# Forgetting attention in an encoder block: two heads at a time on the two halves of the TensorE array

## What is computed

```
scale = q.shape[-1] ** -0.5
cum = jnp.cumsum(log_f, axis=-1)
for blk in range(s // Q_BLOCK):            # Q_BLOCK = 128, s = 512
    lo = blk * Q_BLOCK
    hi = lo + Q_BLOCK
    logits = (einsum("bhtd,bhsd->bhts", q[:, :, lo:hi], k[:, :, :hi]) * scale
              + (cum[:, :, lo:hi, None] - cum[:, :, None, :hi]))
    mask = (lo + arange(Q_BLOCK))[:, None] >= arange(hi)[None, :]
    p = softmax(where(mask, logits, -inf), axis=-1)
    outs.append(einsum("bhts,bhsd->bhtd", p, v[:, :, :hi]))
```

## Time and profile before

| | us |
|---|---|
| median of three runs | 819.95 |
| profiled execution, span from first to last instruction | 818.3 |
| TensorE busy | 805.7 (98%) |
| VectorE busy | 371.3 (45%) |
| ScalarE busy | 255.4 (31%) |
| attention stage, from the first L1319 to the last gate piece | 95.1 |

### The profile page before, as it was taken

The page is one execution under the profiler, slowest core; times in us unless marked ns, Lnnn a source line. Parts: engine busy times, 40 slices in busy tenths (PEclk is TensorE's granted clock), DMA queues, the critical chain, the costliest instruction groups (busy, mean ns, idle before and its releaser), DMA issues.

```text
span 818.3 us, 9506 instructions
## 1 busy us (share of the span) xinstructions
PE 805.7 (98%) x3851; PEld 652.7 (80%) x3851; DVE 371.3 (45%) x573; ACT 255.4 (31%) x421; POOL 24.0 (3%) x43
## 2 busy tenths in 40 slices
PE   6999999999999999999999999999999999999996
PEld 6988887888665578888888988888888888888885
DVE  4688334357654443424435534434443443323224
ACT  6444211343433323323324333322333223213211
POOL 4000000012000000000000000000000000000001
PEclk9999999999999999999999999999999999999999
DMA  8434342311010103533331333322233332331402
GB/s 225 126 99 145 103 129 77 103 52 31 22 52 1 52 1 103 206 103 103 103 103 52 92 115 103 103 89 80 90 102 103 104 103 83 123 103 52 155 0 103
DMA packets 61915, 75.63 MB, mean 92 GB/s; under 512 B 3680, under 2 KB 49840, under 8 KB 61872
## 3 DMA queue, kind: packets, MB, share of 16 engines
q1 hardware_dynamic: 61872, 75.02, 28.9%
HBM read 72.92 MB, written 2.10 MB: 92 GB/s over the span
## 4 chain that ended last, share of the span: by engine, by line
PE 94%; DMA 2%; DVE 1%; issue 1%; ACT 1%; SPq 0%; POOL 0%; POOLq 0%; ACTq 0%; DVEq 0%
PE bank L1136 27%; PE bank L1138 27%; PE bank L1137 27%; PE bank L1319 3%; PE bank L1339 3%; PE bank L1260 2%; DMA x_nat<-in_x 1%; PE bank L1327 1%; PE bank L1299 1%; DMA stage<-in_w_in 1%; PE bank L1286 1%; DVE work L783 0%; DVE w_lo L722 0%; PE bank L1279 0%; PE bank L1148 0%
## 5 line engine op out<-in xcount | busy, mean ns | idle before, releaser
L1136 PE MATMUL bank<-hT_hi,w_hi 128*128 128x512 f32 (+1 forms) x680 | 261.6, 385 | 2.7 <-DVE hT_lo L706 2.5
L1138 PE MATMUL bank<-hT_hi,w_lo 128*128 128x512 f32 (+1 forms) x680 | 257.1, 378 | 0.0
L1137 PE MATMUL bank<-hT_lo,w_hi 128*128 128x512 f32 (+1 forms) x680 | 257.0, 378 | 0.0
L722 DVE TENSOR_TENSOR w_lo<-stage,w_hi 128x1024 fp32r<-128x1024 f32 x125 | 152.4, 1224 | 223.0 <-ACT w_hi L464 214.3
L464 ACT ACTIVATE w_hi<-stage 128x1024 fp32r<-128x1024 f32 x127 | 133.3, 1052 | 132.8 <-PE bank L1138 125.5
L1136 PEld LDWEIGHTS bank<-hT_hi,w_hi 128*128 128x128 f32 x680 | 128.9, 190 | 26.1 <-POOL w_lo L407 2.8
L1138 PEld LDWEIGHTS bank<-hT_hi,w_lo 128*128 128x128 f32 x680 | 128.7, 189 | 23.7
L1137 PEld LDWEIGHTS bank<-hT_lo,w_hi 128*128 128x128 f32 x680 | 128.8, 189 | 21.6
L1136 PE MATMUL bank<-w_hi,aT_hi 128*128 128x512 f32 x176 | 68.5, 389 | 0.0
L1137 PE MATMUL bank<-w_lo,aT_hi 128*128 128x512 f32 x176 | 68.5, 389 | 0.0
L1138 PE MATMUL bank<-w_hi,aT_lo 128*128 128x512 f32 x176 | 68.5, 389 | 0.0
(11 more groups left out here) (169 smaller groups left out, 821.3 us busy)
## 6 DMA issues: line engine op xcount, KB each, us to landing
stage<-in_w_in SPq DMA_DIRECT2D x21, 1024.0 KB, 5.2
stage<-in_w_gate SPq DMA_DIRECT2D x11, 1024.0 KB, 5.3
stage<-in_w_up SPq DMA_DIRECT2D x11, 1024.0 KB, 5.3
stage<-in_w_down SPq DMA_DIRECT2D x22, 512.0 KB, 4.4
stage<-in_w_out SPq DMA_DIRECT2D x4, 1024.0 KB, 5.0
x_nat<-in_x SPq DMA_DIRECT2D x4, 512.0 KB, 5.4
stage<-in_w_br_mlstm SPq DMA_DIRECT2D x4, 512.0 KB, 3.5
stage<-in_w_br_fox SPq DMA_DIRECT2D x4, 512.0 KB, 4.6
```

Source lines behind the costliest of these rows:

```text
L722: dve.tensor_tensor(ring(w_lo, g), staged(g), ring(w_hi, g).bitcast(F32), ALU.subtract).then_inc(lo_split, 1)
L1136: pe.matmul(o, a_hi, b_hi, start=first, stop=False)
L1137: pe.matmul(o, a_hi, b_lo, start=False, stop=False)
L1138: return pe.matmul(o, a_lo, b_hi, start=False, stop=last)
```

## The change

Units are replaced by 16 pairs v: the two heads of a head pair for one query block. `fox_pair(v)` goes through q = 0, 1, 2, 3, 3, 2, 1, 0 twice. For a pair TensorE issues both query-key products (head 0 on array rows 0 to 63, head 1 on rows 64 to 127, into two banks), both row products, and both masks; then, per key block, the value products of the two heads in turn. The row product now uses 64 array rows as well: `rows_both` is copied to partitions 64 and up (three VectorE copies, `rows_low_half`), and `pick` gets a second set of ones by two more `affine_select` on GpSimd (N_CONSTS 17 to 19). There are four `probs` tiles, four logit banks (4, 5, 6, 1), one result bank (0) for all head pairs, and the last head's transpose moves from bank 1 to bank 7. Each pair has two gate pieces from v = 2 on, so 28 of the 32 lie in the loop and 4 behind it; before it was 31 and 1.

```diff
-            def fox_logits(u):
-                hp, q, h2 = fox_unit(u)
...
-                bank, n = 4 + u % 3, (q + 1) * P
-                head = slice(h2 * DH_F, (h2 + 1) * DH_F)
-                take(bank, (fox_exp, u + 1))
-                pe.matmul(psum[bank][:, 0:n], q_f[head, hp, q * P:(q + 1) * P], k_f[head, hp, 0:n], start=True, stop=False)
-                spread_row(bank, H_M + 2 * hp + h2, q, False, True).then_inc(logits, 1)
+            def fox_logits(v):
+                hp, q = fox_pair(v)
+                if v == 0:
...
+                    pe.wait_ge(rows_low_half, 3)
...
+                for h2 in range(2):
+                    take(logit_bank(2 * v + h2), (fox_exp, 2 * v + h2 + 1))
+                for h2, head in enumerate(heads):
+                    pe.matmul(banks[h2][:, 0:n], q_f[head, hp, q * P:(q + 1) * P], k_f[head, hp, 0:n],
+                              start=True, stop=False)
+                for h2, head in enumerate(heads):
+                    lane = H_M + 2 * hp + h2
+                    pe.matmul(banks[h2][:, 0:n], pick[head, lane:lane + 1].to_broadcast([DH_F, P]), rows_both[head, cols],
+                              start=False, stop=False)
+                for h2 in range(2):
+                    pe.matmul(banks[h2][:, q * P:n], ident_b[:, :], mask_b[:, :], start=False,
+                              stop=True).then_inc(logits, 1)
...
+            def fox_values(v):
+                hp, q = fox_pair(v)
...
+                for h2 in range(2):
+                    pe.wait_ge(fox_PT[h2], v + 1)
+                if v % ROWS == 0:
+                    take(0, (yfT_lo_ready, hp + 1))
                 for j in range(q + 1):
-                    last = pe.matmul(psum[hp % 2][h2 * DH_F:(h2 + 1) * DH_F, q * P:(q + 1) * P],
-                                     v_f[:, j, c:c + DH_F], work[u % 2][:, j * P:(j + 1) * P],
-                                     start=(j == 0), stop=(j == q))
+                    for h2 in range(2):
+                        c = (2 * hp + h2) * DH_F
+                        last = pe.matmul(psum[0][h2 * DH_F:(h2 + 1) * DH_F, q * P:(q + 1) * P],
+                                         v_f[:, j, c:c + DH_F], work[h2][:, j * P:(j + 1) * P],
+                                         start=(j == 0), stop=(j == q))
                 last.then_inc(fox_pv, 1)
...
-            for u in range(2, 35):
...
+            for v in range(FOX_PAIRS):
+                fox_transpose(v)
+                if v + 2 < FOX_PAIRS:
+                    fox_logits(v + 2)
+                if v == 0:
+                    mlstm_transpose(3)
+                if v >= FILL_FROM:
+                    gate_piece(2 * (v - FILL_FROM))
+                fox_values(v)
+                if v >= FILL_FROM:
+                    gate_piece(2 * (v - FILL_FROM) + 1)
```

VectorE, at granule `G_MV + 2`, behind the three subtractions that finish `rows_both`:

```diff
+                    for n, (a, b) in enumerate(ROW_CHUNKS):
+                        dve.wait_ge(rows_lo_ready, n + 1)
+                        dve.tensor_copy(rows_both[HALF_ARRAY:HALF_ARRAY + LO + LANES, a * P:b * P],
+                                        rows_both[0:LO + LANES, a * P:b * P].bitcast(F32)).then_inc(rows_low_half, 1)
```

VectorE, the attention stage (ScalarE's loop goes by pairs in the same way, with `take_yfT_hi` and the gate's `tanh` at the head of an iteration):

```diff
+            fox_row_max(0)
+            head_mean_square(3)
+            fox_divide(0)
+            fox_row_max(1)
+            head_normalise(3)
+            take_ymT(2)
+            for v in range(FOX_PAIRS):
+                fox_take_even(v)
+                if v >= ROWS and v % ROWS == 0:
+                    take_yfT_lo(v // ROWS - 1)
+                if v + 1 < FOX_PAIRS:
+                    fox_divide(v + 1)
+                if v + 2 < FOX_PAIRS:
+                    fox_row_max(v + 2)
+                if v == 0:
+                    open_gate(3)
+                if v == 1:
+                    take_ymT(3)
+                if v in (2, 3):
+                    split_lo(G_BR + v)
+                if v in (6, 10):
+                    split_lo(G_BR + 4 + (v - 6) // 4)
```

More of the change, by code:

```diff
@@ L195, in block_kernel @@
         rows_both = at("rows_both", [P, 10 * P], F32R, R + 72 * K)
-        probs = [at(f"probs{i}", [P, SEQ], F32, R + 82 * K + 2 * K * i) for i in range(3)]
+        probs = [at(f"probs{i}", [P, SEQ], F32, R + 80 * K + 2 * K * i) for i in range(4)]
         mo_half_tanh = at("mo_half_tanh", [P, SEQ], F32, R + 70 * K)
@@ L399, in _ @@
                                      base=0, pattern=[[1, P]], channel_multiplier=-1))
+            for at_row in (HALF_ARRAY, HALF_ARRAY + LO):
+                const(pool.affine_select(out=pick[:, H_M:LANES], in_=pick[:, H_M:LANES].bitcast(F32),
+                                         compare_op=ALU.not_equal, fill=1.0, base=-at_row - H_M,
+                                         pattern=[[-1, H_F]], channel_multiplier=1))
+                pool.wait_ge(consts, steps[0])
             assert steps[0] == N_CONSTS
@@ L592, in _ @@
             act.wait_ge(decay_exp, 10 * H_M)
[L593 to L608, removed]
-                if n in (0, 1) and (u - FILL_FROM) % KD == 2:
-                    split_hi(G_BR + 4 + n)
-                if u in (6, 8):
-                    split_hi(G_BR + 2 + (u - 6) // 2)
-                if u >= 8 and u % 8 == 4:
-                    take_yfT_hi(u // 8 - 1)
+            fox_softmax(0)
+            fox_softmax(1)
+            mo_tanh_of(3)
+            take_ymT_hi(2)
+            act.wait_ge(y_m, H_M)
+            for v in range(FOX_PAIRS):
+                if v >= ROWS and v % ROWS == 0:
+                    take_yfT_hi(v // ROWS - 1)
+                if v > FILL_FROM and v % 4 == FILL_FROM:
+                    first_gate_tanh(v // 4 - 1)
+                fox_take_odd(v)
+                if v in (2, 3):
+                    split_hi(G_BR + v)
+                if v + 2 < FOX_PAIRS:
+                    fox_softmax(v + 2)
+                if v == 1:
+                    take_ymT_hi(3)
+                if v in (6, 10):
+                    split_hi(G_BR + 4 + (v - 6) // 4)
             take_yfT_hi(KB - 1)
@@ L987, in fox_take_even @@
+            def fox_take_even(v):
+                _, q = fox_pair(v)
                 n = (q + 1) * P
[L988 to L990 removed]
+                dve.wait_ge(fox_T, 2 * v + 1)
+                if v >= 1:
+                    dve.wait_ge(fox_pv, v)
                 dve.tensor_copy(work[0][:, 0:n], psum[2][:, 0:n]).then_inc(fox_PT[0], 1)
[L993 to L1006 removed]
+            fox_row_max(0)
@@ new lines, in fox_logits @@
+                n = (q + 1) * P
+                cols = slice(pair(q, 0) * P, pair(q, 0) * P + n)
+                banks = [psum[logit_bank(2 * v + h2)] for h2 in range(2)]
+                heads = [slice(h2 * DH_F, (h2 + 1) * DH_F) for h2 in range(2)]
+                for h2 in range(2):
[3 more added lines that the diff above has]
+                              start=True, stop=False)
@@ new lines, in fox_logits, with fox_transpose @@
+                for h2, head in enumerate(heads):
+                    lane = H_M + 2 * hp + h2
+                    pe.matmul(banks[h2][:, 0:n], pick[head, lane:lane + 1].to_broadcast([DH_F, P]), rows_both[head, cols],
+                              start=False, stop=False)
+                for h2 in range(2):
+                    pe.matmul(banks[h2][:, q * P:n], ident_b[:, :], mask_b[:, :], start=False,
+                              stop=True).then_inc(logits, 1)
+            def fox_transpose(v):
+                _, q = fox_pair(v)
+                for h2 in range(2):
+                    u = 2 * v + h2
+                    pe.wait_ge(fox_norm, 2 * u + 2)
+                    take(2 + h2, (fox_PT[h2], v + 1))
+                    for j in range(q + 1):
+                        last = pe.transpose(psum[2 + h2][:, j * P:(j + 1) * P], probs[u % 4][:, j * P:(j + 1) * P], ident[:, :])
+                    last.then_inc(fox_T, 1)
```

155 lines of the change are left out of this document (59 added, 96 removed).

## The result

| | before | after |
|---|---|---|
| median of runs, us | 819.87 (4 runs) | 797.97 (4 runs, 797.34 to 798.50) |
| ratio to before | | 0.9733, 95% interval 0.9722 to 0.9744 |
| profiled execution, span | 818.3 | 796.5 (run time 798.42) |
| attention stage | 95.1 | 73.5 |

The account below looks back on a forecast made before the run. The prediction took TensorE's own instruction list as the bound. Its terms, -5.9 - 3.6 - 2.3 - 6.9 + 2.5 + 0.5 = -15.7 us, brought the span from 818.3 to 802.6, forecast as 804 for a run, range 798 to 818.

Parts of the forecast that it names:

- What bounds the kernel: Whole kernel and attention stage: only TensorE's own list can give time; TensorE is busy for 805.7 of 818.3 us.
- Term 1: Attention units: array shape changes fall from 96 to 64 at 0.184 us each, saving 5.9; counted by fixed parts, 8.8.
- Term 2: Query-key products on two row halves: four slots become three, saving 4.3, less 0.7 for weight loads: net 3.6 us.
- Term 3: Row products: the first head's stands beside the second head's last query-key instruction, saving 2.3 of 4.6 us.
- Term 4: Value products in turn on two column halves: 4(q + 1) slots become 2(q + 1) + 1, saving 6.9 us.
- Term 5: Start of the attention stage: TensorE waits for bank 1 and VectorE's chain, costing 2.5 us (bounds 0 to 4).
- Item 6: Steady state of the pairs: VectorE's work is covered by TensorE's; only the gate tanh at v = 14 costs 0.5 us.
- Item 7: Three VectorE copies at 79 us and two more GpSimd constants: cost 0; without cover 1.6 and 0.6 us.
- The rival with two slots: Query-key and value products: the pair runs as one, two slots instead of three; 799 us, chance 0.04.
- The other side: Logits and values: every change of half costs like a change of shape; 837.5 us, 827 at half price; chance 0.12.

Follow-up runs that it names:

- e8: The kernel after, with the two row products of a pair on all 128 array rows instead of on halves; 800.34 us.
- e1: The kernel after, with a pair's value products issued head by head instead of in turn; 801.58 us.
- e3: The kernel after, with query-key and row products of both heads taken from array rows 0 to 63 (second head's logits wrong); 808.31 us.
- e2: The kernel after, with value products of both heads sent to the same 64 columns (attention result wrong); 805.60 us.
- e7: The kernel after, with value products issued in groups of two key blocks per head; 798.44 us.
- e5: The kernel after, with ScalarE's tanh of bank 3 ahead of pair 1's exponentials and pair 1's logits behind all four pieces of that block; 798.02 us.
- e9: e5's order, with VectorE's starting list changed (division before mean square, head 2's step behind the first copy) and the last head's transposes one pair later; 798.05 us.
- e10: e5's order with pair 0's division ahead of the mean square, gate pieces from pair 0 on, and the last two mLSTM heads' transposes moved off bank 7; 799.48 us.
- e12: e10 with VectorE's copy for the first values ahead of the last mLSTM head's normalise step, and ScalarE's gate tanh ahead of its result copy; 796.17 us.
- e11: The kernel after, unchanged, run again on the same chip as e10; 798.49 us.

## Why the prediction was right and wrong

- **What bounds the kernel**: right. Nearly all of the gain is TensorE's list in that stage.
- **Term 1, changes of shape** (-5.9): right in kind. By the rows after, a pair has 0.21 fixed in the logits, 0.15 in the values, and 0.09 to 0.11 at each of three borders to full-array work: about 0.65 where two units had 1.11, so -7.3 over 16 pairs. No run takes this part away alone; the stage without waits and half clock fell by 27.2, of which terms 2 to 4 as measured below are 19.5, which leaves 7.7. The term counted four changes at one price, and the return ahead of the bf16 mask is cheaper than ahead of the row product (0.21 against 0.31; e8).
- **Term 2, query-key products** (-3.6): the step that failed. "TensorE starts in order: A1, then A2 beside B1, then B2. Four slots become three." The first instructions of both heads start together (two by 213.75 us, above), and e1 shows for the column halves that a start does not wait for earlier ones of the other half. So four slots become two: 17.1 to 8.5, -8.5. The correction of 0.7 for weight loads was wrong too: one-block pairs take 0.48 to the mask, on the same line of 0.27 per block as the others, and loads of two halves go side by side. e3 shows the size: +10.6 for this and the row products, or 11.0 by its rows at full clock, 10.8 expected.
- **Term 3, row products** (-2.3): right by e8 and by e3's 0.27 per block.
- **Term 4, values** (-6.9): the same step, 2(q + 1) slots instead of 2(q + 1) + 1, 80 in all instead of 96: -8.7; e2 gave 8.4 back.
- **Term 5, waits at the start** (+2.5): found the bank 1 wait (1.1 forecast, 1.3 measured) and not the one behind it: bank 3 is also the bank of pair 0's odd transposes, and its tanh stands behind exponentials that wait for VectorE. That is 2.0 us at 209.27. The values then waited less: pair 0's did not wait, since TensorE came to them at 212.69 and their copy was done by 210.6. Sum 3.5. What no term had is the half clock, 1.5: pair 2's logits took 1.91 us (209.61 to 211.52) where the same in e2 took 1.02, and the transposes behind them 0.98 instead of 0.54. By the two lists of VectorE it is three mLSTM steps, not four, that the first copy newly stands behind (L943, L874, L876); the mean square stood ahead of it before as well.
- **Item 6** (+0.5 at pair 14): 0.4, by the row of L588. Elsewhere 0.2 of small waits. **Item 7** (0): right, the stage even starts 0.2 earlier.

Sum with the measured sizes: -7.3 - 8.5 - 2.3 - 8.7 + 3.5 + 1.5 + 0.6 = -21.2 against -21.8. Of the terms' errors -1.4, -4.9 and -1.8 stand against +2.6.

The rival with two slots was there, with the right place and about the right time (799), and had 0.04. Its chance was low because the order of a product's two instructions was taken for a rule, which no row showed; nothing in the trace of before bears on the order between halves. The range should have reached down to that case with all of term 1 by its other count (8.8), 796. The other side, a change of half that costs, is out: sixteen alternating instructions take no longer than eight of one half did.

## What to carry to other kernels

When two small products lie on different halves of the array, price them as one. Their issue order can be loose: three instructions of the other half in between cost next to nothing (e7), seven cost more than half of the overlap (e1). When a stage becomes a fifth shorter, look for the first moment at which the engine has nothing to do, in every bank that its next instructions take, and bring work there, not only a better order; reordering alone (e5, e9) renamed the wait, work alone (e10) gathered it, both (e12) took half of it away. Price TensorE's waits with what may follow in the clock: here 1.5 us behind 3.2 us of waits, in some executions and not in others.

## What the runs showed of the hardware

- Products on the two row halves and on the two column halves of the array ran fully side by side in float32 (1.02 us for 16 value instructions, 1.89 on one half), and so did their weight loads.
- Starts on the two column halves are not strictly in the order of the list: in e1 head 1's group began while three instructions of head 0, earlier in the list, were still to start (16 instructions in 1.51 us; 1.08 in e7).
- Behind waits of 1.3 and 2.0 us (from 203.0 to 209.3) the granted clock fell to 0.50, for 3.4 us in each of the profiles of after, of its second run e11 and of e1 and e7, in e9 as long behind other waits, and for 20.5 us in e3, whose waits (0.9 and 1.4) were shorter. e2, with waits of 1.3 and 2.0, e8 with 1.0 and 1.7, and e10 with one of 2.5 show no fall. Executions of one kernel differ too: e8's slowest took 803.1 us at a mean granted clock of 0.990, its three others 799.9 to 800.4 at 0.996 and 0.997. What decides whether and how long stays open; it was not tried.
